# Float32r triples for most projections and the output product of the two mixers of a two-block transformer kernel

## The reference, cut to what matters

```python
h = _rmsnorm_2(x) * (1.0 + sc2) + sh2
x = x + g2 * _hybrid_mixer(h, w_in[l], w_out[l], ...)

def _hybrid_mixer(h, w_in, w_out, ...):
    proj = h @ w_in                      # 256 x 1024 @ 1024 x 3584
    qa, ka, va, qd, kd, vd, qh, fh, ih, gh = jnp.split(proj, offsets, axis=-1)
    o_a = _stick_breaking(qa, ka, va)
    o_d = _dilated_mixture(rope(norm(qd)), rope(norm(kd)), vd)
    log_f = logaddexp(log(lb), log1p(-lb) + log_sigmoid(fh))
    o_h = _hgrn2_chunkwise(silu(qh), -expm1(log_f), ih, log_f)
    o_h = _rmsnorm_2(o_h) * hgrn_norm_g * silu(gh)
    return concatenate([o_a, o_d, o_h]) @ w_out      # 256 x 1024 @ 1024 x 1024
```

## Time and profile before

| | |
|---|---|
| three runs | 1743.59, 1746.66, 1747.12 us; median 1746.66 |
| profiled execution | 1745.78 us, of which the profile's span is 1743.7 us |
| granted clock, mean | 0.952 of full speed |
| PE matmuls busy | 1574.5 us, 90% of the span |
| DVE / ACT / POOL busy | 979.8 / 602.9 / 203.9 us |
| chain that ended last | PE 73%, DVE 10%, ACT 6%, POOL 2% of the span |
| first mixer, second mixer | 742.2 to 911.5 us, 1360.1 to 1529.4 us |

### The profile page before, as it was taken

One profiled execution on the slowest core, in us unless ns is written; L12 is line 12 of the kernel. 1 busy time (PEld: TensorE's weight loads), 2 busy tenths in 40 slices (PEclk: granted clock), 3 DMA queues, 4 the chain that ended last, 5 costly groups with the idle time before them and its releaser, 6 DMA issues.

```text
span 1743.7 us, 21727 instructions
## 1 busy us (share of the span) xinstructions
PE 1574.5 (90%) x8944; PEld 1237.1 (71%) x8944; DVE 979.8 (56%) x1482; ACT 602.9 (35%) x944; POOL 203.9 (12%) x205
## 2 busy tenths in 40 slices
PE   6978759899788998999998998989999999989998
PEld 1635536645648997786548997779987875579986
DVE  0257585767527777445336777667774453354444
ACT  2214311142115443353125443244433541244442
POOL 0020341100000110014000110001100251001100
PEclk9999969998699999999998999989999999989999
DMA  9324224236245888432345886838876222355651
GB/s 343 114 96 148 94 73 146 73 139 260 97 157 193 267 281 305 150 121 73 98 138 168 284 290 247 320 127 285 283 288 213 97 97 97 97 160 178 194 170 48
DMA packets 192105, 305.44 MB, mean 175 GB/s; under 512 B 6139, under 2 KB 116487, under 8 KB 191879
## 3 DMA queue, kind: packets, MB, share of 16 engines
q1 hardware_dynamic: 189088, 299.45, 50.7%
q10 hardware_dynamic: 2919, 4.61, 0.7%
HBM read 302.99 MB, written 1.05 MB: 174 GB/s over the span
## 4 chain that ended last, share of the span: by engine, by line
PE 73%; DVE 10%; issue 6%; ACT 6%; DMA 2%; POOL 2%; ACTq 0%; DVEq 0%; POOLq 0%
PE ps L373 71%; DVE accs L514 2%; PE ps L376 1%; DVE wlo L1940 1%; ACT whi L1898 1%; DMA ring<-in_w_mod_dram 1%; DMA ring<-in_ffn_w_down_dram 1%; DVE arena L1197 1%; DVE arena L1194 1%; DVE H L1787 1%; DVE H L1721 1%; ACT arena L1432 0%; DVE misc L1499 0%; POOL misc L1768 0%; ACT hhi L1903 0%
## 5 line engine op out<-in xcount | busy, mean ns | idle before, releaser
L1940 DVE TENSOR_TENSOR wlo<-ring,whi 128x1024 fp32r<-128x1024 f32 x264 | 322.7, 1225 | 235.4 <-ACT whi L1898 230.0
L373 PE MATMUL ps<-hhi,whi 128*128 128x256 f32 x1408 | 407.4, 289 | 22.9 <-DVE hlo L1946 16.7
L373 PE MATMUL ps<-hlo,whi 128*128 128x256 f32 x1408 | 403.8, 287 | 0.0
L373 PE MATMUL ps<-hhi,wlo 128*128 128x256 f32 x1408 | 403.7, 287 | 0.0
L1898 ACT ACTIVATE whi<-ring 128x1024 fp32r<-128x1024 f32 x264 | 275.2, 1055 | 309.5 <-PE ps L373 277.5
L373 PEld LDWEIGHTS ps<-hhi,whi 128*128 128x128 f32 x1408 | 275.8, 196 | 24.9 <-DVE hlo L1946 23.7
L373 PEld LDWEIGHTS ps<-hlo,whi 128*128 128x128 f32 x1408 | 275.7, 196 | 1.2 <-issue 1.2
L373 PE MATMUL ps<-ring,H 128*128 128x512 f32 (+1 forms) x608 | 266.2, 589 | 11.0 <-ACT arena L2075 5.5
L373 PEld LDWEIGHTS ps<-hhi,wlo 128*128 128x128 f32 x1408 | 275.5, 196 | 0.0
L373 PEld LDWEIGHTS ps<-ring,H 128*128 128x128 f32 x608 | 115.1, 196 | 131.2 <-issue 115.8
L514 DVE SCALAR_TENSOR_TENSOR accs<-ring,misc,accs 128x512 f32<-128x512 f32 x266 | 201.1, 756 | 3.0
(11 more groups left out here) (288 smaller groups left out, 1402.6 us busy)
## 6 DMA issues: line engine op xcount, KB each, us to landing
ring<-in_w_mod_dram SPq DMA_DIRECT2D x84, 1024.0 KB, 7.3
ring<-in_w_in_dram SPq DMA_DIRECT2D x48, 1024.0 KB, 5.1
ring<-in_ffn_w_gate_dram SPq DMA_DIRECT2D x44, 1024.0 KB, 6.8
ring<-in_ffn_w_up_dram SPq DMA_DIRECT2D x44, 1024.0 KB, 5.4
ring<-in_ffn_w_down_dram SPq DMA_DIRECT2D x44, 1024.0 KB, 6.6
ring<-in_w_out_dram SPq DMA_DIRECT2D x12, 1024.0 KB, 4.8
gates<-in_b_mod_dram SPq DMA_DIRECT2D x7, 512.0 KB, 6.4
ring<-in_w_proj_a_dram SPq DMA_DIRECT2D x2, 1024.0 KB, 5.9
```

The lines of the kernel that those rows point to most:

```text
L373: return self.e.matmul(o, lhsT, rhs, start=start, stop=stop)
L1940: v.done(v.e.tensor_tensor(lo, M.slot(key)[:, r0:r0 + rn, :], plain(hi), ALU.subtract), ("split", l, sub, n), *([M.freed(key)] if ends els ...
```

## The change

- `SPLIT` names the projection steps that become float32r triples: 4 to 11 (qh; qa and ka), 20 to 27 (ih and gh), and 28 to 35, which are eight pieces of the output product, one for each 128 rows of w_out. So eight of the twelve feature steps, two of the four token projections and all of the product are split; steps 0 to 3 and 12 to 19 stay plain.
- A piece n is 128x1024. ACT writes its high part (`act_high`) into one of four buffers (n % 4), which lie over `gates`, `accs`, `wlo` and `ahi`; POOL or DVE (`low_weights`) writes the low part in place into the ring's slot. POOL has pieces 4 to 11 and the odd ones from 21 on (`ON_POOL`), DVE the even ones from 20 on.
- In `in_steps` ACT makes the high part of piece s + 3 at the start of step s, and DVE its low part at the end of step s. POOL's low parts stand ahead of its levels (4 to 11) and between its later operations.
- The high part of piece n waits until PE is done with piece n - 4 (`staged`).
- The normalized input is split as well: four copies on ACT, four subtractions on DVE, 128x512 each. The transposed result is split by ACT (`YHI`) and DVE (`v_turned`, `YLO`).
- The feature steps rotate over six PSUM banks instead of two. The squares of the norm go to another buffer and don't wait for `modps`. Three loads of gates' biases in layer 1 wait for the first mixer's residual.

Core of the diff (line numbers of the changed file in the order excerpts differ from those before):

```diff
+SPLIT = (*range(4, 12), *range(20, 36))
+ON_POOL = (*range(4, 12), *range(21, 36, 2))
...
-    ends = {2: ("residual", "first"), 5: ("residual", 0, 0), 8: ("residual", 0, 1)}
+    ends = {2: ("residual", 0, 1), 5: ("residual", 0, 1), 8: ("residual", 0, 1)}
...
+def act_high(a, l, n):
+    M = a.M
...
+    key, w, _, _ = weights(M, l, n)
+    a.wait_ge(key, ("staged", l, 1, n - 12 if n in range(20, 24) else n - 4))
+    a.done(a.e.activation(split_weights(M, l, n)[1], w, ACT.Copy), ("whi", l, 1, n))
...
+def low_weights(lane, l, n):
+    M = lane.M
+    _, hi, lo, _ = split_weights(M, l, n)
+    lane.wait_ge(("whi", l, 1, n))
+    lane.done(lane.e.tensor_tensor(lo, weights(M, l, n)[1], plain(hi), ALU.subtract), ("split", l, 1, n))
...
+def act_highs(a, l):
+    for n in range(3, 31):
+        if n in SPLIT:
+            act_high(a, l, n)
+        yield
...
+def v_lows(v, l):
+    for n in range(3, 31):
+        if n in SPLIT and n not in ON_POOL:
+            low_weights(v, l, n)
+        yield
...
-def in_steps(lane, l, proj, rec, stick, dil, first):
+def in_steps(lane, l, proj, rec, stick, dil, first, ahead, behind):
...
     for step in range(28):
+        tick(ahead)
         if first:
             tick(proj)
...
         if not first:
             tick(proj)
+        tick(behind)
...
-            b = pe.bank(("f", l, name, j), "proj")
-            pe.wait_ge(key)
+            b = pe.bank(("f", l, name, j), "feat")
+            key, hi, lo, ends = split_weights(M, l, n)
+            pe.wait_ge(("split", l, 1, n) if n in SPLIT else key)
             for kt in range(8):
...
+                if n in SPLIT:
+                    pe.wait_ge(("hlo", l, 1, kt // 4))
+                    ins = pe.mm3(b[:, 0:256], (hi[:, kt, :], lo[:, kt, :]), (M.MHI[:, kt, :], M.MLO[:, kt, :]), kt == 0, kt == 7)
...
         g.done(g.e.memset(flat(t), 0.0), ("zero", l))
+    for n in range(4, 12):
+        low_weights(g, l, n)
     for lv in range(3):
         pool_level(g, l, lv)
...
+    low_weights(g, l, 21)
     pool_rstd(g, ("k", l), 8)
+    for n in (23, 25, 27):
+        low_weights(g, l, n)
     pool_rstd(g, ("y", l), 8)
+    for n in (29, 31, 33, 35):
+        low_weights(g, l, n)
...
-            key, n = ("out", name, 2 * kp), OUTS.index(kp)
-            pe.wait_ge(key, ("yt", l, kp))
+            at = OUTS.index(kp)
+            n, c = 28 + 2 * at + k, slice(blk * 128, (blk + 1) * 128)
+            key, hi, lo, ends = split_weights(M, l, n)
+            pe.wait_ge(("split", l, 1, n), ("yt", l, kp))
...
+    act_high(a, l, 31)
     act_dilated_end(a, l)
-    for kp in (2, 3, 1):
-        act_turned(a, l, kp)
+    act_turned(a, l, 2)
+    act_turned(a, l, 3)
+    for n in (32, 33, 34, 35):
+        act_high(a, l, n)
+    act_turned(a, l, 1)
```

More of the change, by code:

```diff
@@ L180, in __init__ @@
         self.X = self.sb("X", [128, 2, 1024])
-        self.gates = self.sb("gates", [128, 4, 1024])
-        self.accs = self.sb("accs", [128, 2, 512])
-        self.H = self.sb("H", [128, 8, 512])
+        self.gates, self.gates_r = self.twice("gates", [128, 4, 1024])
+        self.accs, self.accs_r = self.twice("accs", [128, 2, 512])
+        self.H, self.H_r = self.twice("H", [128, 8, 512])
         self.mc2 = [self.sb(f"mc2_{l}", [128, 72]) for l in range(2)]
@@ L197, in sb, with twice @@
         return self.ctx.enter_context(self.nc.sbuf_tensor(name, shape, f32))
+    def twice(self, name, shape):
+        with self.nc.sbuf_tensor(name, shape, f32) as plain_:
+            pass
+        return plain_, self.sbr(f"{name}_r", shape)
     def sbr(self, name, shape):
@@ L236, in slot, with slot_r @@
         return self.ring[:, n % NS, 0:a * b].rearrange("p (a b) -> p a b", b=b)
+    def slot_r(self, key):
+        n, a, b = self.slots[key]
+        return self.ring_r[:, n % NS, 0:a * b].rearrange("p (a b) -> p a b", b=b)
     def freed(self, key):
@@ L2369, in act_turned, with v_turned @@
     a.wait_ge(key, ("lq", l, 7), ("diag", l, 1))
-    a.done(a.e.activation(M.YT[:, 2 * kp:2 * kp + 2, :], M.ps(key).rearrange("p (k t) -> p k t", k=2), ACT.Copy), ("free", key), ("yt", l, kp))
+    a.done(a.e.activation(M.YHI[:, 2 * kp:2 * kp + 2, :], M.ps(key).rearrange("p (k t) -> p k t", k=2), ACT.Copy), ("yhi", l, kp))
+def v_turned(v, l, kp):
+    M, key = v.M, ("turn", l, kp)
+    v.wait_ge(("yhi", l, kp))
+    v.done(v.e.tensor_tensor(M.YLO[:, 2 * kp:2 * kp + 2, :], M.ps(key).rearrange("p (k t) -> p k t", k=2),
+                             plain(M.YHI[:, 2 * kp:2 * kp + 2, :]), ALU.subtract), ("free", key), ("yt", l, kp))
 def act_stick(a, l):
```

109 lines of the change are left out of this document (92 added, 17 removed).

## The result

| | before | after |
|---|---|---|
| median, four runs each | 1746.48 us | 1759.01 us (1758.62 to 1760.8) |
| ratio, with its 95% interval | | 1.0077 (1.006 to 1.0094) |
| profiled execution, its span | 1745.78, 1743.7 us | 1758.66, 1756.9 us |
| mean granted clock | 0.952 | 0.939 |
| first mixer, to the first matmul of the next stage | 172.08 us | 178.94 us |

The forecast was 1741.9 us, within 1726 to 1752; the change is 0.8% slower. Both mixers lose 6.9 us, 13.8 in all; the profiled execution as a whole lost 12.9, since its first mixer began 3.9 us earlier and the stages between the mixers took 3.3 us more.

The account below looks back on a forecast made before the run. PE was taken to bound the mixer. Each mixer would lose 6.1 us in the feature steps and gain 8.5 from step 20 on: 2.4 us a mixer, 4.8 in all, giving 1741.9 us, range 1726 to 1752.

Parts of the forecast that it names:

- ACT's late high parts 9 to 11: Feature steps: ACT makes these high parts only after the gate chain's four Exps, ending at 775.8, 776.9 and 777.9.
- PE's idle time before piece 9: Feature steps: PE idles from 770.5 to 778.6, about 8 us, until POOL's low part 9 is done.
- The gap before the product: Before the output product: PE idles 3.4 us instead of 1.31, as low 29 on POOL holds DVE's subtraction; 2.1 us more.
- the key's rotation: Last third: the rotation on DVE waits for low parts, so PE's transposes come 1.2 us after PE could.
- The gain on PE, if nothing waits: Whole mixer: 4.6 us from features, 5.9 from ih and gh, 5.9 from the product; 16.4 us a mixer.
- rival (c): POOL's low part costs 2.96 us, so a mixer loses 3.7 us; 1754.1 us in all, chance 0.15.
- PE, done with piece 10 by about 786.2, does the level's scores at 789.6: Feature steps: level 0's scores start when DVE's products for it end, at 789.6 instead of 782.92.
- piece 12: After the feature steps: piece 12 starts at 795.95 instead of 789.89, 6.1 us later.
- rival (d): PE's clock halves after idling: hidden at piece 9, 1.7 us a mixer lost before the product; 1745.3 us, chance 0.15.
- POOL's low part: On POOL: a low part of 128x1024 takes 1.95 us, within bounds of 1.89 to 2.96.
- A float32r triple of 128x512: Projections and product on PE: 0.680 us for 0.865 plain, saving 0.185 us on each matmul.
- The rule weighed: POOL holds only DVE instructions with two SBUF operands; were all held, some 2 us a mixer more, 1745.9 us.

Follow-up runs that it names:

- e11: The change with feature pieces 4 to 11 plain and the low part of piece 29 on DVE instead of POOL; 1730.94 us, ratio 0.9923 to before.
- e13: The change with DVE's two diagonal masks moved ahead of the products of level 1; 1747.35 us, ratio 1.0015 to before.
- e3: The change with constant matmuls filling PE's idle time, nine before piece 9 and three before level 0's scores; 1757.89 us, ratio 1.0064 to before.
- e12: e7 with only the output product split (pieces 28 to 35), its first four high parts waiting for steps 8 to 11; 1734.01 us, ratio 0.9937 to before.
- e7: The change with plain features, all low parts from step 20 on DVE, high 30 behind the Silu copy of gh; 1724.43 us, ratio 0.9891 to before.
- e15: e14 with high part 9 on ACT at once behind high 8; 1740.49 us, ratio 0.998 to before.
- e14: e13 with POOL's level 0 behind low 9 and its level 1 behind low 10; 1747.78 us, ratio 1.0019 to before.

## Why the prediction was wrong

**What held.** The shape of the loss in the feature steps: ACT's late high parts 9 to 11, PE's idle time before piece 9 (8.69 for 8), POOL as its releaser, DVE's operations that read three microseconds beside a low part, high parts that hide elsewhere. The gap before the product (3.61 for 3.4), with its cause (low 29, shown by e11), and the key's rotation (1.02 for 1.2). The gain on PE, if nothing waits, as a direction. That rival (c), with 1754.1, lies nearest to the measured time is luck: its low part of 2.96 us was not there.

**The step that failed first** is "PE, done with piece 10 by about 786.2, does the level's scores at 789.6". The operands were indeed ready at 784.6, +46.3, a little before the forecast +47.4, as only the first of level 0's two products was held by POOL (1.65 us, then 0.68). But scores also need a PSUM bank, and the bank was freed by a mask that stands behind the products of the next level in DVE's order. Before, the masks ended just as PE finished piece 10, so that the earlier trace rows show no wait there. The row of DVE before (two masks, from 781.54 to 782.8, with the scores at 782.92):

```profile
781.54 1.28 DVE L2255 TENSOR_TENSOR arena<-ps,ctab 128x512 f32<-128x512 f32 x2
```

The change made the levels' chain late and PE early, and so turned a hidden order into the bound: PE, free at +47.0 and with its operands there since +46.3, waits until +49.8, and what follows runs at the lower clock. With the order mended (e13) piece 12 stands at +53.4 to +54.0, where the prediction's other terms put it, at +53.7. That they meet so well is in part luck: the operands came 1.1 us earlier than forecast, and PE was through with piece 10 3.0 us later (+47.0 for +44.0), mostly because piece 9 ran at the lower level. The prediction walked the operands of each step and never asked for its bank.

**The step that failed second** is rival (d), the clock, made a rival where it belonged into the sum. It was judged hidden at piece 9, rightly (piece 9 took 5.26 us, from 775.23 on, and e3 shows that this costs nothing). It was not charged at all behind the wait before level 0's scores, where the lower level takes 3.44 us for the scores instead of 1.73 and 4.13 for piece 11 instead of 2.88: 3.0 us. It was taken as an aside before the product (1.7 us; measured: the first stretch takes 8.37 us where the second takes 5.65, so 2.7), and left out behind the two short waits at the key and before step 24, where step 24 took 4.22 instead of 2.87 us: 1.4. (The 4.60 us that rival (d) reads from the earlier trace rows are moreover those of the second row behind the idle time, not of the first.) So of the 5.6 us missing from step 20 on some 4.1 are clock. On the other side, 1.7 us of the low stretch of before were not there.

**Terms mis-sized.** POOL's low part: 2.37 us, forecast 1.95. The nearest row chosen was a level with a broadcast operand, and the choice was wrong. The Trainium skill, "GPSIMD Engine Reference", section "3.1 Elementwise — side-by-side cycle accounting", gives 4.5 us for the addition of two float32 tensors of 2048 elements per partition; half of it is 2.25, an estimate, nearer to the 2.37 of these rows than the row was. Rival (c) had 2.35 as the point where the forecast's gain is used up, but reckoned the scores from their operands as well; these came at +46.3, earlier than forecast in spite of that price, so it is not what decided. A float32r triple of 128x512 in the mixer: starts are 0.23 us apart in a row, and a stretch of 24 took 5.65 us (897.11 to 902.76) where 5.44 was forecast, a step of 12 2.87 for 2.72. That makes 5.3 and 5.2 us a mixer for the product and for ih with gh (e12, e7) instead of 5.9 each.

**The sum.** Per mixer, forecast -2.4, measured +6.9, so 9.3 missing. Piece 12: +11.5 late for 6.1, 5.4 us, of them the bank with the clock behind it. Piece 12 to step 20: 1.7 gained by the clock. From step 20: 5.6, of them 4.1 clock and 1.3 the triples' price (5.9 less 5.3, and 5.9 less 5.2). 5.4 - 1.7 + 5.6 = 9.3. By cause this is 2.5 for the bank (by which the scores start later than forecast), 5.4 for the clock (3.0 + 4.1 - 1.7) and 1.3 for the triples; some 0.1 stays without a cause. So the bank came first in time, and through the clock behind it cost more than its own wait; but the clock is the larger of the two terms that the sum left out.

**The rule weighed** in the prediction held. The row of POOL's low 35 and DVE's reduction beside it, in the kernel after:

```profile
884.75 2.84 POOL L2092 TENSOR_TENSOR ring_r<-ring,ahi 128x1024 fp32r<-128x1024 f32 x1 [6.48 <-ACT ahi L2085]
```

```profile
885.38 1.22 DVE L2670 TENSOR_REDUCE misc<-arena 128x4 f32<-128x1024 f32 x1
```

The reduction, with one operand in SBUF, takes the 1.22 us that it takes in the kernel before as well, while DVE's operations with two wait (3.31 for 1.23 us beside low 8). That is what the Trainium skill, "SBUF — State Buffer", section "Who interferes with whom", states of operations with one SBUF input; this trace agrees.

**Still open:** which waits the lower clock follows (two mixers with the same waits had one low stretch and three, e3), and with it why the clock is low less often in e15 than in e14. Filling PE's idle times in the mended order was not tried.

## What to carry to other kernels

A step waits for its operands and for the place where its result goes: for each step that a change makes late or early, ask who frees its bank or buffer, and what stands ahead of that instruction in its engine's order. Work on a helper engine is priced with its hold on the neighbour's chain: one 2.4 us subtraction on POOL beside a DVE operation whose result PE waits for lengthened that operation from 1.23 to 3.13 us, and PE's wait from 1.72 to 3.62, where doing the subtraction on DVE took 1.2. To a wait of PE belongs the half-speed work that may follow it: in this kernel 1.3 to 3 us behind waits of 1.6 to 3.6 us, where no later wait hid it. It is a term of the sum with a chance, not an aside.

## What the runs showed of the hardware that was not expected

- Waits as short as 1.02 and 1.60 us, whose ends are 2.2 us apart, were followed by work at the lower level (step 24 of the kernel after: 4.22 us for 2.87). Of the profiled mixers that have both waits 14 of 20 show it, of the 16 that have the 1.60 us alone none. Behind the 3.6 us before the product all 18 show it, behind the wait of 2.40 us 18 of 38 (before both, after neither). Two mixers of one execution with the same waits differ by 3.5 us (e3).
- POOL and DVE alternate at instruction boundaries: DVE read 3.31 us (2.1 waited, 1.2 worked) with low 8, in e15 twice in a row, and POOL 3.01 (after) and 3.40 us (e15) for its 2.37 where DVE was ahead.
- High parts on ACT, one behind the other, start 0.95 us apart for 1.04 us each (pieces 9 to 11 of the kernel after).
